# Two sums over four tiles in the branch stage: added on GpSimd first, then one product with ones

## The reference, cut to what matters

```python
def sgu_branch(p, ln_g, ln_b, w_s, b_s):
    z = jax.nn.gelu(p, approximate=False)
    u, v = jnp.split(z, 2, axis=-1)
    mean = jnp.mean(vf, axis=-1, keepdims=True)
    var = jnp.mean(jnp.square(vf - mean), axis=-1, keepdims=True)
    v = ((vf - mean) * lax.rsqrt(var + EPS) * ln_g + ln_b).astype(p.dtype)
    ...
    mixed = jnp.einsum('gij,bnjgd->bnigd', w, vc) + b_s.T[:, :, None]
    return u * mixed.reshape(B, S, SG_WIDTH)
```

## Time and profile before

| | |
|---|---|
| time, median of 3 runs | 3456.91 us (3454.43, 3456.91, 3463.46) |
| profiled execution, its own time | 3468.01 us |
| its span | 3466.2 us |
| mean granted clock of PE | 0.977 |
| PE busy | 3339.1 us, 96% |
| DVE busy | 1893.7 us, 55% |
| ACT busy | 1434.7 us, 41% |
| POOL busy | 58.5 us, 2% |

### The profile page before, as it was taken

One profiled execution on the slowest core, in us unless ns is written; L12 is line 12 of the kernel. 1 busy time (PEld: TensorE's weight loads), 2 busy tenths in 40 slices (PEclk: granted clock), 3 DMA queues, 4 the chain that ended last, 5 costly groups with the idle time before them and its releaser, 6 DMA issues. The chain is left out here.

```text
span 3466.2 us, 53876 instructions
## 1 busy us (share of the span) xinstructions
PE 3339.1 (96%) x21860; PEld 2612.1 (75%) x21860; DVE 1893.7 (55%) x3265; ACT 1434.7 (41%) x2357; POOL 58.5 (2%) x44
## 2 busy tenths in 40 slices
PE   8999999999999999999999999899899999999898
PEld 6777688788877876887888778566587787566686
DVE  6645644677566446346773552367555632376555
ACT  6423423444254235234443333545533333555532
POOL 0110000000000100000000000000000000000000
PEclk9999999999999999999999999899999999999999
DMA  4324232223232233322233252122152432121341
GB/s 157 95 67 172 101 116 89 91 95 111 86 131 89 76 127 138 114 85 98 96 106 101 103 166 89 40 89 77 47 179 95 154 115 104 51 74 59 129 138 67
DMA packets 106534, 356.86 MB, mean 103 GB/s; under 512 B 12545, under 2 KB 12929, under 8 KB 103489
## 3 DMA queue, kind: packets, MB, share of 16 engines
q1 hardware_dynamic: 106304, 353.67, 30.0%
HBM read 308.93 MB, written 38.80 MB: 100 GB/s over the span
## 5 line engine op out<-in xcount | busy, mean ns | idle before, releaser
L224 PE MATMUL banks<-h_high,weights_high 128*128 128x512 f32 x2464 | 993.2, 403 | 27.8 <-DVE weights_low L245 19.9
L225 PE MATMUL banks<-h_low,weights_high 128*128 128x512 f32 x2464 | 969.3, 393 | 0.0
L226 PE MATMUL banks<-h_high,weights_low 128*128 128x512 f32 x2464 | 968.4, 393 | 0.0
L224 PEld LDWEIGHTS banks<-h_high,weights_high 128*128 128x128 f32 x2464 | 466.5, 189 | 141.4 <-DVE weights_low L245 21.2
L226 PEld LDWEIGHTS banks<-h_high,weights_low 128*128 128x128 f32 x2464 | 466.3, 189 | 102.6
L225 PEld LDWEIGHTS banks<-h_low,weights_high 128*128 128x128 f32 x2464 | 467.0, 190 | 97.1 <-issue 3.3
L217 DVE TENSOR_TENSOR weights_low<-ring,weights_high 128x1024 fp32r<-128x1024 f32 x134 | 167.1, 1247 | 304.4 <-ACT weights_high L212 303.6
L1689 ACT CAST weights_high<-ring 128x1024 fp32r<-128x1024 f32 (+2 forms) x124 | 140.7, 1134 | 456.8 <-PE banks L226 456.4
L1737 DVE TENSOR_TENSOR weights_low<-ring,weights_high 128x1024 fp32r<-128x1024 f32 (+2 forms) x124 | 164.6, 1327 | 294.3 <-ACT weights_high L1689 294.2
L212 ACT CAST weights_high<-ring 128x1024 fp32r<-128x1024 f32 x134 | 140.4, 1048 | 367.4 <-PE banks L226 362.3
L1865 ACT CAST weights_high<-ring 128x1024 fp32r<-128x1024 f32 (+1 forms) x116 | 132.6, 1143 | 334.4 <-PE banks L226 334.4
(11 more groups left out here) (454 smaller groups left out, 5057.0 us busy)
## 6 DMA issues: line engine op xcount, KB each, us to landing
ring<-in_in SPq DMA_DIRECT2D x136, 512.0 KB, 3.7
ring<-in_up SPq DMA_DIRECT2D x88, 512.0 KB, 3.2
ring<-in_gates SPq DMA_DIRECT2D x68, 512.0 KB, 3.7
x<-in_gates SPq DMA_DIRECT2D x60, 512.0 KB, 3.9
ring<-in_down SPq DMA_DIRECT2D x32, 704.0 KB, 4.1
ring<-in_out SPq DMA_DIRECT2D x32, 512.0 KB, 3.2
ring<-in_branch SPq DMA_DIRECT2D x16, 768.0 KB, 4.4
stored<-g_spill SPq DMA_DIRECT2D x16, 768.0 KB, 4.5
```

The lines of the kernel that those rows point to most:

```text
L224: pe.matmul(bank, core.wh[:, half, w], high, start=start, stop=False)
L225: pe.matmul(bank, core.wh[:, half, w], low, start=False, stop=False)
L226: return pe.matmul(bank, core.wl[:, half, w], high, start=False, stop=stop)
```

## The change

The four tiles are added pairwise on POOL, in v's place, and PE takes one product of their sum; the same for the squares. A new semaphore `sg_summed` tells PE; `own_pool` lets POOL wait for its own adds.

```diff
-            pe.wait_ge(sems["sg_activated"], 1)
             pe.wait_ge(sems["score_out"], 2 * NCH)
-            for m in range(4):
-                mm = pe.matmul(banks[2][:, :], core.ones[:, :], sg_v[:, m, :], start=(m == 0), stop=(m == 3))
-            mm.then_inc(sems["sg_mean_mm"], 1)
+            pe.wait_ge(sems["sg_summed"], 1)
+            pe.matmul(banks[2][:, :], core.ones[:, :], v[:, 0, :], start=True, stop=True).then_inc(sems["sg_mean_mm"], 1)
...
                 if c == 1:
-                    for m in range(4):
-                        pe.wait_ge(sems["sg_squared"], m + 1)
-                        mm = pe.matmul(banks[3][:, :], core.ones[:, :], sg_squares[:, m, :], start=(m == 0), stop=(m == 3))
-                    mm.then_inc(sems["sg_var_mm"], 1)
+                    pe.wait_ge(sems["sg_summed"], 2)
+                    pe.matmul(banks[3][:, :], core.ones[:, :], v[:, 2, :], start=True, stop=True).then_inc(sems["sg_var_mm"], 1)
...
+        @block.gpsimd
+        def _(pool):
+            own = Own(pool, sems["own_pool"])
+
+            pool.wait_ge(sems["v_mm"], NCH)
+            pool.wait_ge(sems["sg_activated"], 1)
+            own(pool.tensor_tensor(v[:, 0, :], sg_v[:, 0, :], sg_v[:, 1, :], ALU.add))
+            own(pool.tensor_tensor(v[:, 1, :], sg_v[:, 2, :], sg_v[:, 3, :], ALU.add))
+            own.settle()
+            pool.tensor_tensor(v[:, 0, :], v[:, 0, :], v[:, 1, :], ALU.add).then_inc(sems["sg_summed"], 1)
+            for n in range(2):
+                pool.wait_ge(sems["sg_squared"], 2 * n + 2)
+                own(pool.tensor_tensor(v[:, 2 + n, :], sg_squares[:, 2 * n, :], sg_squares[:, 2 * n + 1, :], ALU.add))
+            own.settle()
+            pool.tensor_tensor(v[:, 2, :], v[:, 2, :], v[:, 3, :], ALU.add).then_inc(sems["sg_summed"], 1)
```

More of the change, by code:

```diff
@@ L1289, in branches @@
                "own_act", "sg_activated", "sg_mean_mm", "sg_squared", "sg_var_mm", "sg_rooted", "sg_normed", "sg_t_mm", "sg_t_out",
-               "masked", "mix_mm", "mixed", "rw_done") as (block, sems):
+               "masked", "mix_mm", "mixed", "rw_done", "sg_summed", "own_pool") as (block, sems):
         @block.sync
```

## The result

The change is slower: 3468.75 us, median of 15 runs (3460.14 to 3476.88), against 3461.01 us for the kernel before in 15 runs (3454.43 to 3467.32). The ratio is 1.0023, 95% interval 1.0015 to 1.0030: 7.7 us, between 5 and 10. The prediction had 3.8 us, and it started from the median of the three runs shown, 3456.91, which lies 4.1 us under the median of fifteen. The two errors together put the measured median 8.05 us above the forecast and 1.75 us above the range.

A forecast was written before the change was run, and what follows sets the result against it. PE was taken to bound the kernel, with DVE its equal at the mean sum. Per layer 0.0 + 0.3 + 1.7 = 2.0 us, unrounded 3.8 us slower for two, on 3456.9 gave 3460.7 us; range 3448 to 3467.

The forecast's parts named there:

- What bounds: Whole kernel: PE, busy 96% of the span, bounds it; DVE is its equal from 346.65 to 368 us.
- the mean sum: Layer's mean products: POOL's adds make DVE 2.5 us late, so the 2.65 us saved come back; gain 0.0 us.
- the three waits: PE waits 0.5 us before the mean product, 1.4 before the next gate blocks, 0.7 before the c = 1 state product.
- The variance sum: Variance product: PE pauses 2.9 us for POOL's last add; the product ends 0.3 us later a layer.
- the second rival: Variance sum: DVE's next L1255 goes before POOL's last add, PE's pause 4.1 us; 6.4 or 9.8 us slower; chance 0.22.
- The first rival: Both sums: DVE is not held up; 4.2 us a layer saved, 3448.5 us; chance 0.13 with what lies between.
- The clock: Behind the variance pause PE falls to 1.2 GHz for one 3.4 us spell a layer, a loss of 1.7 us.
- both layers run alike: Layer 1 repeats layer 0, 965.25 us later, so one layer was worked out and doubled.
- The bound I gave: Clock loss a layer behind the variance pause: between 0 and 3.4 us, the latter for a spell twice as long.
- my rule: PE at the lower clock level: 3.4 us do half the work, a loss of 1.7 us.
- The base: Whole kernel: the starting time was the median of the runs shown, 3456.9 us; the three runs span 9 us.
- No change: Whole kernel: measured time within 0.3% of before; chance 0.87, against 0.04 for faster and 0.09 for slower.

The follow-up runs named there:

- The first experiment: The change with only the mean sum added on POOL and the variance sum as four products again: 3462.6 us, ratio 1.0007 to the kernel before.

## Why the prediction was right or wrong, point by point

**What bounds, and the mean sum: right.** DVE was the pace between 346 and 362. From the gelu, L1576 (before: L1564) stands at 20.13 us, where it was 17.80: DVE is 2.33 us late, predicted 2.5. Of the three waits forecast with 0.5, 1.4 and 0.7 us, PE shows pauses of 0.18, 0.96 and 0.55. They look shorter mostly because I counted from start to start and the profile counts from the end of the last product's record, which is longer than the spacing of two. Counted my way they are 0.35, 1.38 and 0.64 us, and the first is short because DVE was less late. The place where they end, the state product of c = 1, is 0.28 us earlier than before, predicted 0.03. The first experiment has this 0.29 us by itself.

**The variance sum: right.** Pause 2.82 us (2.9), ended by POOL; the last add began 0.1 us ahead of the next L1255 (0.15 forecast), so the second rival did not come true. That was close enough to have gone the other way. Without the clock the state product of c = 2 would stand at about 30.96, where the run with the pause filled has it: 0.23 us later than before, predicted 0.3. The first rival (DVE not held up) is excluded by the durations of L1255, L1515 and L1517.

**The clock: the step that failed, by its size.** "I take one such spell a layer" of 3.4 us, worth 1.7 us. That the clock falls was right, and layer 0 has the spell: of its 1.65 us, about 1.4 are clock (61.30 against 59.89 with the pause filled). Layer 1 has a spell of 10.2 us, three times as long: 64.33 against 59.90, 4.4 us of clock. That "both layers run alike, so I work out one and double it" holds for the pauses (2.82 and 2.83 us) but not for what the clock does behind them. The bound I gave, twice as long and 3.4 us, was too near as well. The trace of before has spells of 10.2 us, at 404.7 and 1370.7, at pauses of 7.4 us; 5 to 6 us of each lie behind the pause's end. The clock term should have been 5.8 us for the two layers, not 3.3, and the ratio 1.0018, inside the measured interval. Why the same pause is followed by 3.4 us in one layer and 10.2 us in the other, in both profiles, stays open. So does why 10.2 us at the lower level cost 4.4 us and not half, 5.1 us, as my rule would give. (My sum is also a little uneven: 3.4 us at half speed are 1.7 us, and I doubled 1.65; with 1.7 it gives 3.9 us.)

**The base.** The forecast of the time took the median of three runs as it was. With 15 it lies 4.1 us higher. I had noted the 9 us between the three but not widened the range for it; by a base of 3461.0 the forecast would have been 3464.8 and the range up to 3471, with the measured 3468.75 inside. The 2.5 us that the clock term lacked would have brought the forecast to 3463.2 and the 4.1 us of the base to 3467.3; the last 1.4 us are what the medians show above the two phases, within their interval. The 7.7 us also lie between the two sums of the second rival, 6.4 and 9.8 us, but not by its way: the last add did not wait again.

**Signs and chances.** No change (within 0.3%) had 0.87 and is what came, at 0.23% (0.15 to 0.30), on the slower side as worked out.

## What to carry to other kernels

In this kernel the work that was moved to GpSimd and reads SBUF was paid for by what VectorE did at that moment with two SBUF inputs. Look at what VectorE is the pace of just then, not at its average, and move the sum for which VectorE has room. Here the variance sum alone was worth nearly its full 2.65 us a layer (ratio 0.9980), and both sums together cost 0.2%. A product removed from TensorE in front of a wait only makes the wait longer, and a pause of 2.8 us cost more in clock in one layer (4.4 us) than the products that it replaced: keep TensorE at work, or place the product behind something that it can do first.

## What the runs showed of the hardware that was not expected

- A pause of PE of 2.8 us was followed by 3.4 us at 1.2 GHz in one layer and by 10.2 us in the other, in both profiles of the change. PE was busy for all of the 10.2 us.
- Filling that pause with products whose results are thrown away kept the clock up in the phase in all four layers profiled, and made the kernel 5.5 us faster by the means of twelve runs each on one chip (1.5 to 9.5), with six products more (three a layer).
- POOL's write-only memsets of 128x512 took 0.53 us beside DVE and held nothing, where the adds took up to 2.26 us and held DVE's operations 0.7 to 1.1 us each.
